# Start addresses of the low weight slots in a hand-scheduled two-block transformer kernel

## Time and profile before

| | |
|---|---|
| median of three runs | 1046.15 us |
| the profiled execution | 1045.56 us |
| its span, first to last instruction | 1043.8 us |
| TensorE matmuls (PE) | 1029.9 us busy, 99% of the span, 8398 matmuls |
| TensorE weight loads (PEld) | 975.5 us, 93% |
| VectorE (DVE) / ScalarE (ACT) / GpSimd (POOL) | 719.3 / 573.0 / 286.9 us |
| DMA | 180.11 MB, 173 GB/s on average |
| granted clock of TensorE | 0.999 of full speed |

### The profile page before, as it was taken

The page is one execution under the profiler, slowest core; times in us unless marked ns, Lnnn a source line. Parts: engine busy times, 40 slices in busy tenths (PEclk is TensorE's granted clock), DMA queues, the critical chain, the costliest instruction groups (busy, mean ns, idle before and its releaser), DMA issues.

```text
span 1043.8 us, 20017 instructions
## 1 busy us (share of the span) xinstructions
PE 1029.9 (99%) x8398; PEld 975.5 (93%) x8398; DVE 719.3 (69%) x1217; ACT 573.0 (55%) x791; POOL 286.9 (27%) x179
## 2 busy tenths in 40 slices
PE   8999999999999999999999999999999999999997
PEld 7999998999999899999999989998999999899996
DVE  5762248798688776322788967877888789766763
ACT  6555465655355544445765534556657875343443
POOL 0386675100000137666740000013400035101120
PEclk9999999999999999999999999999999999999999
DMA  9644454565763665344455566457432257663841
GB/s 307 200 160 158 144 183 162 163 199 174 233 202 127 202 226 173 122 162 132 159 194 176 189 216 223 137 153 220 123 111 96 62 183 230 194 211 128 258 170 41
DMA packets 169705, 180.11 MB, mean 173 GB/s; under 512 B 4240, under 2 KB 166416, under 8 KB 169488
## 3 DMA queue, kind: packets, MB, share of 16 engines
q1 hardware_dynamic: 169616, 178.84, 53.5%
HBM read 177.78 MB, written 1.05 MB: 171 GB/s over the span
## 4 chain that ended last, share of the span: by engine, by line
PE 81%; DVE 8%; ACT 4%; POOL 4%; issue 2%; DMA 1%; SPq 0%; POOLq 0%; ACTq 0%; DVEq 0%
PE psum L686 80%; DVE sb_w_lo L1868 3%; ACT sb_scratch L1336 2%; POOL sb_w_lo L2622 1%; POOL sb_scratch L2653 1%; ACT sb_w_hi L1336 1%; DVE psum L1852 1%; DVE sb_xg_lo L1852 1%; DVE sb_scratch L1852 1%; POOL sb_scratch L2662 1%; DMA sb_raw<-in_w_in 1%; PE psum L913 1%; DVE sb_xt L1886 0%; ACT L1336 0%; DVE sb_xt L1884 0%
## 5 line engine op out<-in xcount | busy, mean ns | idle before, releaser
L1336 ACT ACTIVATE sb_w_hi<-sb_raw 128x2048 fp32r<-128x2048 f32 (+3 forms) x185 | 318.4, 1726 | 156.4 <-PE psum L686 92.3
L686 PE MATMUL psum<-sb_xg_hi,sb_w_hi 128*128 128x256 f32 x1656 | 393.8, 280 | 0.6 <-DVE psum L1852 0.4
L686 PE MATMUL psum<-sb_xg_lo,sb_w_hi 128*128 128x256 f32 x1656 | 388.8, 277 | 0.0
L1868 DVE TENSOR_TENSOR sb_w_lo<-sb_raw,sb_w_hi 128x2048 fp32r<-128x2048 f32 (+3 forms) x150 | 305.7, 2042 | 101.6 <-ACT sb_w_hi L1336 100.7
L686 PEld LDWEIGHTS psum<-sb_xg_hi,sb_w_hi 128*128 128x128 f32 x1656 | 310.3, 187 | 4.4 <-DVE sb_xg_lo L1852 1.0
L686 PEld LDWEIGHTS psum<-sb_xg_lo,sb_w_hi 128*128 128x128 f32 x1656 | 310.5, 188 | 0.3
L686 PE MATMUL psum<-sb_xg_hi,sb_w_lo 128*128 128x256 f32 x1656 | 227.8, 280 | 1.0 <-DVE sb_w_lo L1868 1.0
L686 PE MATMUL psum<-sb_hid_both,sb_w_hi 128*128 128x512 f32 (+1 forms) x912 | 210.2, 364 | 0.8 <-DVE sb_hid_both L1943 0.6
L686 PEld LDWEIGHTS psum<-sb_xg_hi,sb_w_lo 128*128 128x128 f32 x1656 | 208.5, 187 | 2.0 <-DVE sb_w_lo L1868 1.4
L2622 POOL TENSOR_TENSOR sb_w_lo<-sb_raw,sb_w_hi 128x2048 fp32r<-128x2048 f32 (+1 forms) x34 | 156.0, 4594 | 106.3 <-ACT sb_w_hi L1336 97.0
L686 PEld LDWEIGHTS psum<-sb_hid_both,sb_w_hi 128*128 128x128 f32 x912 | 148.5, 188 | 22.2 <-DVE sb_hid_both L1943 1.4
(11 more groups left out here) (172 smaller groups left out, 969.9 us busy)
## 6 DMA issues: line engine op xcount, KB each, us to landing
sb_raw<-in_w_in SPq DMA_DIRECT2D x51, 1024.0 KB, 5.2
sb_raw<-in_w_up SPq DMA_DIRECT2D x44, 1024.0 KB, 5.1
sb_raw<-in_w_ff SPq DMA_DIRECT2D x21, 1024.0 KB, 5.6
sb_raw<-in_w_down SPq DMA_DIRECT2D x16, 768.0 KB, 4.9
sb_raw<-in_w_down SPq DMA_DIRECT2D x16, 640.0 KB, 4.5
sb_raw<-in_w_out SPq DMA_DIRECT2D x8, 1024.0 KB, 5.3
sb_raw<-in_w_ff SPq DMA_DIRECT2D x8, 768.0 KB, 4.9
sb_raw<-in_w_ff SPq DMA_DIRECT2D x8, 640.0 KB, 4.5
```

Source lines behind the costliest of these rows:

```text
L686: return nc.tensor.matmul(ps, lhsT, rhs, start=start, stop=stop, skip_group_check=True)
L1336: return nc.scalar.activation(out_, in_, func, **kw)
L1868: v.tensor_tensor(part(w_lo, s), part(raw, s), part(w_hi, s).bitcast(F32), ALU.subtract)\
```

## The change

The gaps ahead of the three `w_lo` buffers become 8, 16 and 8 columns, where they were 40, 0 and 192.

```diff
         w_hi = slots("w_hi", (88, 128, 128), F32R)
-        w_lo = slots("w_lo", (40, 0, 192), F32R)
+        w_lo = slots("w_lo", (8, 16, 8), F32R)
```

## The result

Five runs of the changed kernel have a median of 1049.98 us (1049.69 to 1051.18), five of the kernel before 1046.19. The ratio is 1.0038, with a 95% interval of 1.0027 to 1.0048: the change costs 0.4%, where a gain of 0.2% was forecast. The profiled execution took 1049.79 us.

The account below looks back on a forecast made before the run. TensorE was taken to bound the kernel; slot 2's -2.8, 0 for slots 0 and 1, and -0.2 us sum to -3.0, times 0.81 is -2.4, so 1043.7 us against 1046.15; range 1038.5 to 1054.

Parts of the forecast that it names:

- What bounds the kernel: TensorE has a matmul in flight for 1029.9 of 1043.8 us; a saving there counts for about 0.81 of itself.
- That the distance between what streams and what loads sets the step: On TensorE, distance modulo 512 bytes sets the pace: low loads 116.7 ns at 224 and 480, high 113.3 at 64.
- The rival by which nothing happens: TensorE's low pace belongs to something other than the address, or slot effects cancel: 1046.2 us; chance 0.14.
- The prices of slots 0 and 1: Low loads moved from 224 to 96 and 160 bytes stay at 116.7 ns, so 0 us for each slot.
- The rival with all three at the floor: Low loads at 96 and 160 are as good as at 64; all three slots save, 1039.0 us; chance 0.20.
- Slot 2 at 113.3: Slot 2's low loads, moved from 480 to 192 bytes, drop from 116.7 to 113.3 ns: 2.8 us saved on TensorE.
- Slabs with loaded activations, -0.2 us: 128 low matmuls that load an activation and move low weights, a third with slot 2: 0.2 us saved.
- The slower rival: Low parts at 160 or 192 leave the high matmuls behind them at the slow 118 ns: 1052 us; chance 0.31.
- this rival's 1050.9 for one slow slot: Slower rival's case of one slot setting the slow pace beside two neutral ones: 4.8 us on the time, 1050.9 us.
- No effect on the engines that make the low parts: VectorE's pairs of low parts stay at 4.71 us whatever the address: 0, bound 1.5 us of VectorE's time either way.

Follow-up runs that it names:

- The shifted activations: Against the kernel before, 32 unused columns shift the activations by 128 bytes, with all low slots at distance 96: 1050.71 us in one run.

## Why the prediction was wrong

**What bounds the kernel: right.** A loss of 4.5 us in TensorE's steps became 4.2 us of span in the profiled pair, 0.93 of it, and 3.8 us in the medians (1049.98 - 1046.19), 0.84 of it. The prediction took 0.81; runs of one kernel spread over 1.5 us and more, which can't tell these factors apart.

**That the distance between what streams and what loads sets the step: right.** The shifted activations show it. The rival by which nothing happens falls with it. The Trainium skill, "SBUF — State Buffer", section "Who interferes with whom", gives the moving operand and the weight loads independent read ports and says that TensorE never waits on anyone. Read as a rule for TensorE's own two reads, it doesn't agree with this case: their distance moved a step from 113.3 to 120 ns, and the measurement decides.

**The prices of slots 0 and 1: wrong, and this is the step that failed.** The prediction put the distances into two kinds, multiples of 64 and odd multiples of 32, and gave 96 and 160 "116.7, the price of its kind, so 0". They aren't of one kind. The trace of before had one pace at 224 and 480 only because these two are the same distance modulo 256, so they were a single sample, counted as two. The prediction itself noted that these two lie 256 apart and run alike, used that for 192, and didn't ask what it left of the evidence on 96 and 160. 96 cost 120 (the end of the range that the prediction itself gave, from a `vd` slab), 160 cost 119.6 and another 20 ns in the four highs behind it. What the trace after shows in place of the two zeros is +1.7 us for slot 0 and +2.3 us for slot 1's low steps, with 2.0 more (1.34 + 0.68) in the high parts behind the low ones, most of it behind 160. The rival with all three at the floor rested on the same guess, that 96 is as good as its neighbour 64, and fell with it.

**Slot 2 at 113.3: right in price, half in size.** Its low stretches are 0.91 us. Of the forecast 2.8 us 1.45 came. The low loads of the tiles over `xg` went from 116.7 to 114.1 ns (493 steps behind another low one), but in the tiles whose highs move 512 columns they are in the slow pace: 117.3 ns before, 118.1 after (178 steps, 0.71 and 0.85 us over 113.3). At 192 the low part takes the pace that it finds, and this the prediction named only as the upper bound. In those wide tiles 96 stayed at 117.4 ns (190 steps), so its price of 120 holds for the others only, while 160 went from 117.3 to 119.4 there (176 steps).

**Slabs with loaded activations, -0.2 us: wrong, but too small to matter.** Their low steps took 119.4 ns in slot 2 before and after, and 1.0 and 1.4 ns more than before in slots 0 and 1, together 0.1 us more.

**The slower rival: its mechanism exists, but the change doesn't run into it.** It priced a high part at 118 instead of 113, and that is what 0, 176 and 192 in all slots show. In the kernel after, slots 0 and 1 both bring TensorE back, so only 9 of 154 tiles without a stall are slow (4 before). The loss came mainly from low parts that are slower themselves, and the prediction had no case for that. Its own upper ends for slots 0 and 1 (+2.7 us each) would have turned its sum of -3.0 into +2.4 us; it named these ends and then counted both as 0. That the measured 1049.98 us lies close to this rival's 1050.9 for one slow slot is luck: the work that was slower is another.

**No effect on the engines that make the low parts: right.** 4.71 us before, 4.71 and 4.72 after.

## What to carry to other kernels

Two operands that one engine reads at the same time have a distance between their starts, and on a kernel that is all matmuls a sweep of that distance is worth a look: here it moved the time from -0.1% to +0.6% (in the kernels that were run several times) with no instruction changed. Before two values in a trace are called two samples of a kind, ask whether they are the same value under a shorter period. A slow pace may be kept by the work behind it, so a change of layout is judged over many tiles behind a stall, not in the tile that it touches.

## What the runs showed of the hardware

The step from one matmul of 256 fp32r columns to the next depends on the distance of the stationary operand from the moving one modulo 256 bytes, by what was measured here (mean step from one low matmul to the next, in tiles over `xg`; "back" says that the highs behind return to 113.3 where the tile ahead was slow, "set" that they are slow where it was fast):

| distance | ns a step | highs behind |
|---|---|---|
| 0 | 120 | set to 118 |
| 32 | 118 | slow pace kept behind a slab's first low part, back behind its second |
| 48, 112 | 117.9, 118.5 | back in 21 of 25 cases and in 3 of 7; the first two slow |
| 64 (low parts at 320, and all high parts), 192 | 113.3 or 117.8, as the work ahead | kept as it is |
| 80 | 119 | back |
| 96 | 120 | back |
| 128 | 118.0 | back, two at 122 and 118 |
| 160 | 119.6 | back, four slow by about 20 ns in all |
| 176 | 118.2 | set to 118 |
| 208, 224 | 116.7 | back |
| 240 | 117.9 | back |

No distance was both at 113.3 and back, and the old layout, 224 in all slots (modulo 256), is within 0.1% of the best found. 16 and 144 were not tried. At 64 and 192 TensorE has two stable paces for the same work, 113.3 and 117.8 ns, and a stall is where it goes from the first to the second: in before, 13 of 34 tiles behind a stall. Which stalls do it, and what inside the chip gives each distance its pace, stays open; these runs only show the paces.
